# Attention scores ahead of two U/W tiles, eight PSUM banks in turn, and running sums ahead of the next scores

## The reference

```python
    k_all = jnp.concatenate([P['ak'], Pc['ak']], axis=1)
    o_att = _attend(P['aq'], k_all, v_all)          # softmax(q k' / 8) v
    o_dn, _, _ = _bidir_gdn(P, s_f, s_b)            # starts from the context's states

    # in _chunk_gdn, for chunks of 64 tokens
    u = einsum(tmat, vb)                            # tmat: inverse of (eye + lmat)
    w = einsum(tmat, kb * exp(gc))
    def step(S, inp):
        v_new = u_i - w_i @ S
        o = (q_i * exp(g_i)) @ S + qk_i @ v_new
        S = S * exp(g_last) + (k_i * exp(g_last - g_i)).T @ v_new
```

```python
        log_not = jnp.where(strict, jax.nn.log_sigmoid(-z), 0.0)
        after = lax.cumsum(log_not, axis=3, reverse=True) - log_not
        a = jnp.where(strict, jnp.exp(jax.nn.log_sigmoid(z) + after), 0.0)
        o = a @ v
```

## Time and profile before

| | |
|---|---|
| time, median of 3 runs | 1709.5 us (1709.14 to 1713.87) |
| profiled execution, its own time | 1710.61 us |
| its span in the trace | 1708.8 us |
| PE busy | 1543.9 us, 90% |
| DVE, ACT busy | 881.4 us (52%), 688.3 us (40%) |
| mean granted clock of TensorE | 0.901 |
| first block | 0 to about 640 us |
| loop of the attention and delta net | about 301 to 410 us |
| turns 7 to 11 of the two layers | 809 to 852 us, 1335 to 1381 us |

### The profile page before, as it was taken

How to read it: one execution, slowest core, us unless ns; L and a number is a source line. 1 busy time by engine, 2 the same in 40 slices (tenths; PEclk the granted TensorE clock), 3 DMA queues, 4 the chain that set the end, 5 groups by cost and what they waited for, 6 DMA issues and landing times. The chain is left out here.

```text
span 1708.8 us, 26973 instructions
## 1 busy us (share of the span) xinstructions
PE 1543.9 (90%) x11283; PEld 1305.1 (76%) x11283; DVE 881.4 (52%) x1330; ACT 688.3 (40%) x1141; POOL 75.6 (4%) x87
## 2 busy tenths in 40 slices
PE   4998889999799997989889899996989898899996
PEld 1555668666499997978787799986978787799984
DVE  0542643223455553467567555565448558555555
ACT  2112224323244442347662344453336664244442
POOL 0001661000000000000000000000000000000000
PEclk9888799556899997999999899998899998899998
DMA  9522154000445432622222755532642233555520
GB/s 357 203 70 78 38 198 165 1 1 1 173 172 190 177 101 81 197 99 99 99 99 99 295 196 178 177 125 74 181 159 67 83 119 128 214 200 180 193 99 25
DMA packets 118814, 230.34 MB, mean 135 GB/s; under 512 B 17984, under 2 KB 32448, under 8 KB 117952
## 3 DMA queue, kind: packets, MB, share of 16 engines
q1 hardware_dynamic: 115696, 221.37, 37.3%
q10 hardware_dynamic: 3024, 7.64, 1.2%
HBM read 227.95 MB, written 1.05 MB: 134 GB/s over the span
## 5 line engine op out<-in xcount | busy, mean ns | idle before, releaser
L707 DVE TENSOR_TENSOR work_rounded<-ring,work_rounded 128x1024 fp32r<-128x1024 f32 x208 | 240.8, 1220 | 113.7 <-ACT work_rounded L699 113.5
L670 PE MATMUL psum<-channels_rounded,work_rounded 128*128 128x256 f32 x2048 | 285.7, 286 | 0.9 <-DVE work_rounded L737 0.9
L670 PEld LDWEIGHTS psum<-channels_rounded,work_rounded 128*128 128x128 f32 x2048 | 271.6, 195 | 4.8 <-issue 3.4
L681 PE MATMUL psum<-work_rounded 128*128 128x512 f32 x1152 | 265.7, 390 | 0.0
L923 PE MATMUL psum<-channels_rounded,ring_rounded 128*128 128x256 f32 x1728 | 254.1, 291 | 3.0 <-DVE channels_rounded L1352 3.0
L699 ACT ACTIVATE work_rounded<-ring 128x1024 fp32r<-128x1024 f32 x208 | 203.2, 1050 | 131.7 <-PE psum L681 118.5
L681 PEld LDWEIGHTS psum<-work_rounded 128*128 128x128 f32 x1152 | 214.7, 188 | 43.6
L923 PEld LDWEIGHTS psum<-channels_rounded,ring_rounded 128*128 128x128 f32 x1728 | 230.7, 198 | 5.3 <-DVE channels_rounded L1352 3.8
L1344 DVE TENSOR_TENSOR ring_rounded<-ring,ring_rounded 128x1024 fp32r<-128x1024 f32 x80 | 94.4, 1195 | 61.0 <-ACT ring_rounded L1167 60.8
L1167 ACT ACTIVATE ring_rounded<-ring 128x1024 fp32r<-128x1024 f32 x80 | 80.6, 1024 | 24.3 <-DMA ring<-in_w_in 24.3
L747 DVE TENSOR_TENSOR work<-work 128x512 f32<-128x512 f32 x48 | 33.2, 692 | 109.7 <-ACT work L719 109.7
(11 more groups left out here) (358 smaller groups left out, 2158.6 us busy)
## 6 DMA issues: line engine op xcount, KB each, us to landing
ring<-in_w_in SPq DMA_DIRECT2D x20, 2048.0 KB, 7.8
ring<-in_w_ff SPq DMA_DIRECT2D x16, 2048.0 KB, 8.2
ring<-in_w_ff_in SPq DMA_DIRECT2D x16, 2048.0 KB, 8.0
ring<-in_w_ff_out SPq DMA_DIRECT2D x16, 2048.0 KB, 8.0
ring<-in_w_mod SPq DMA_DIRECT2D x12, 2048.0 KB, 8.6
ring<-in_w_out SPq DMA_DIRECT2D x6, 2048.0 KB, 8.7
ring<-in_w_in SPq DMA_DIRECT2D x8, 1024.0 KB, 5.4
ring<-in_w_up SPq DMA_DIRECT2D x4, 2048.0 KB, 8.0
```

The lines of the kernel that those rows point to most:

```text
L670: mm = pe.matmul(psum[:, 4 + 2 * half + q, i * SEQ:(i + 1) * SEQ], w1[pw][:, k, m * P:(m + 1) * P], y[py][:, k, :], start=((k, n) == (0, 0 ...
L681: mm = pe.matmul(psum[:, 2 * t + n, :], h[ph][:, kq, t * P:(t + 1) * P], w2[pw][:, kq, n * 512:(n + 1) * 512], start=False, stop=False, sk ...
L707: dve.tensor_tensor(parts.low[i % 2][:, at], ring[:, SLOT * s + 1024 * c:SLOT * s + 1024 * (c + 1)], exact(parts.high[i % 2][:, at]), ALU. ...
```

## The change

1. **Banks.** Every job of the first block up to the loop's last, that is all but the catA, catD, g and later ones, is added with `wide=True` and takes bank (4 + n) % 8. `Jobs` remembers who was in each bank last, and a job waits for that one: eight jobs back instead of four. The second block's jobs are as before.
2. **S_0.** The first scores, with the wait for the keys' copy, move on PE from behind the last W to behind the second tile's W, ahead of U and W of tiles 0 and 1. ACT's `probs(0)` moves likewise ahead of its copies of those four jobs. DVE's program is the same there.
3. **Stick-breaking turns.** In turns 7 to 11 the step T of the head before goes ahead of S of the next, on all three engines and in the order of the jobs. DVE's weights and their wait for the exponential move from step V to directly behind the addition in step T.

```diff
@@ class Jobs
+    def add(self, name, by, wide=False):
+        bank = (4 + len(self.all)) % 8 if wide else 4 + len(self.all) % 4
+        job = {"name": name, "n": len(self.all), "by": by, "k": self.counts[by], "bank": bank,
+               "old": self.in_bank.get(bank)}
+        self.in_bank[bank] = name
...
     def before(self, name):
-        n = self.by_name[name]["n"]
-        return self.all[n - 4]["name"] if n >= 4 else None
+        return self.by_name[name]["old"]
@@ first_jobs (every add up to PV15 has wide=True)
-    for t in TILES_D:
+    for n, t in enumerate(TILES_D):
+        if n == 2:
+            j.add("S0", "act", wide=True)
         add("act", f"U{t}", f"W{t}")
-    j.add("S0", "act")
@@ attention_schedule
     for n, (kind, h) in enumerate(HEADS + [(None, None)]):
+        swapped = last and last[:2] == "sb"
+        if swapped:
+            steps.append(("T", last))
         if kind:
             steps.append(("S", f"{kind}{h}"))
-        if last:
+        if last and not swapped:
             steps.append(("T", last))
@@ DVE, step T of a stick-breaking head (the same lines are gone from its step V)
                                     r.read(f"T_{name}", dve.tensor_tensor(b, b, ps, ALU.add))
+                                    dve.wait_ge(sb_exp, h + 1)
+                                    dve.scalar_tensor_tensor(out=b, in0=b, scalar=-1.0, in1=const_a("sb_neg"),
+                                                             op0=ALU.mult, op1=ALU.mult).then_inc(sb_weights, 1)
@@ PE, first block
                     for n, t in enumerate(TILES_D):
+                        if n == 2:
+                            w.after("akT")
+                            scores(0)
                         ps = w.open(f"U{t}")
...
-                    w.after("akT")
-                    scores(0)
                     for n in range(8):
@@ ACT, first block
+                    for n, t in enumerate(TILES_D):
+                        if n == 2:
+                            probs(0)
                         ps = r.open(f"U{t}")
...
-                    probs(0)
                     for n in range(8):
```

More of the change, by code:

```diff
@@ L145, in __init__ @@
         self.all, self.by_name, self.counts = [], {}, {"dve": 0, "act": 0, "gate": 0}
-    def add(self, name, by):
+        self.in_bank = {}
+    def add(self, name, by, wide=False):
         assert name not in self.by_name, name
-        job = {"name": name, "n": len(self.all), "by": by, "k": self.counts[by]}
+        bank = (4 + len(self.all)) % 8 if wide else 4 + len(self.all) % 4
+        job = {"name": name, "n": len(self.all), "by": by, "k": self.counts[by], "bank": bank,
+               "old": self.in_bank.get(bank)}
+        self.in_bank[bank] = name
         self.counts[by] += 1
@@ L154, in bank @@
     def bank(self, name):
-        return 4 + self.by_name[name]["n"] % 4
+        return self.by_name[name]["bank"]
     def full(self, name):
@@ L201, in add @@
         for name in names:
-            j.add(name, by)
+            j.add(name, by, wide=True)
     for u in range(4):
@@ L216, in first_jobs @@
     for kind, t in couplings_order():
-        j.add(f"{kind}{t}", "dve")
+        j.add(f"{kind}{t}", "dve", wide=True)
     for t in TILES_D:
-        j.add(f"LT{t}", "act")
+        j.add(f"LT{t}", "act", wide=True)
     add("act", "AT0", "AT1")
@@ L222, in first_jobs @@
         for t in TILES_D:
-            j.add(f"P{t}{lv}", "dve")
+            j.add(f"P{t}{lv}", "dve", wide=True)
         for n, t in enumerate(TILES_D):
             if lv == 5:
-                j.add(f"INV{t}", "act")
+                j.add(f"INV{t}", "act", wide=True)
                 continue
             if n % 2 == 0:
-                j.add(f"mod{2 + 2 * lv + n // 2}", "act")
+                j.add(f"mod{2 + 2 * lv + n // 2}", "act", wide=True)
             add("act", f"X{t}{lv}", f"XT{t}{lv}")
             if n % 2 == 0:
-                j.add(f"modT{2 + 2 * lv + n // 2}", "dve")
+                j.add(f"modT{2 + 2 * lv + n // 2}", "dve", wide=True)
     add("act", "aqT0", "aqT1", "aqT2", "aqT3", "akT")
-    for t in TILES_D:
+    for n, t in enumerate(TILES_D):
+        if n == 2:
+            j.add("S0", "act", wide=True)
         add("act", f"U{t}", f"W{t}")
-    j.add("S0", "act")
     for n in range(8):
         if n:
-            j.add(f"WS{n}", "dve")
+            j.add(f"WS{n}", "dve", wide=True)
         add("act", f"PT{2 * n}", f"S{2 * n + 1}")
-        j.add(f"SU{n}", "dve")
+        j.add(f"SU{n}", "dve", wide=True)
         if n >= 4:
@@ L245, in first_jobs @@
         if n < 7:
-            j.add(f"S{2 * n + 2}", "act")
-        j.add(f"PV{2 * n + 1}", "act")
+            j.add(f"S{2 * n + 2}", "act", wide=True)
+        j.add(f"PV{2 * n + 1}", "act", wide=True)
     for n in ("catA0", "catA1", "catD", "g0_0", "g0_1", "g1_0", "g1_1"):
@@ L1964, in _, with scores @@
                     w.done(mm)
+                    def scores(i):
+                        h, t = i // 2, i % 2
+                        kvh = half(h // 4)
+                        w.done(pe.matmul(w.open(f"S{i}"), v3(qT1, SEQ)[kvh, h % 4, t * P:(t + 1) * P], kT1[kvh, :],
+                                         start=True, stop=True))
                     for n, t in enumerate(TILES_D):
+                        if n == 2:
+                            w.after("akT")
+                            scores(0)
                         ps = w.open(f"U{t}")
@@ L1980, in _ @@
                         w.done(mm)
-                    def scores(i):
-                        h, t = i // 2, i % 2
-                        kvh = half(h // 4)
-                        w.done(pe.matmul(w.open(f"S{i}"), v3(qT1, SEQ)[kvh, h % 4, t * P:(t + 1) * P], kT1[kvh, :],
-                                         start=True, stop=True))
                     def probs_T(i):
@@ L2225, in _ @@
                     copy("akT", kT1)
-                    for t in TILES_D:
-                        ps = r.open(f"U{t}")
-                        for d in range(2):
-                            for p_ in range(2):
-                                last = act.activation(U_step[step_of[t, d, p_]][half(p_), :],
-                                                      ps[half(p_), 256 * d:256 * d + 256], ACT.Copy)
-                        r.read(f"U{t}", last)
-                        copy(f"W{t}", WT[t])
                     def probs(i):
@@ L2245, in values @@
                         r.read(f"PV{i}", act.mul(aq3[:, t, h * HD:(h + 1) * HD], r.open(f"PV{i}", HD), rden[:, i:i + 1]))
-                    probs(0)
+                    for n, t in enumerate(TILES_D):
+                        if n == 2:
+                            probs(0)
+                        ps = r.open(f"U{t}")
+                        for d in range(2):
+                            for p_ in range(2):
+                                last = act.activation(U_step[step_of[t, d, p_]][half(p_), :],
+                                                      ps[half(p_), 256 * d:256 * d + 256], ACT.Copy)
+                        r.read(f"U{t}", last)
+                        copy(f"W{t}", WT[t])
                     for n in range(8):
```

5 lines of the change are left out of this document (removed).

## The result

| | before | after |
|---|---|---|
| median of four executions | 1711.6 us (1709.14 to 1713.87) | 1661.5 us (1635.31 to 1684.89) |
| profiled execution, its own time | 1710.61 us | 1635.31 us |
| its span | 1708.8 us | 1633.5 us |
| mean granted clock | 0.901 | 0.940 |
| ratio, 95% interval | | 0.9572 (0.953 to 0.9614) |

What parts the groups turned out to be the heart of the matter. Six more executions of the same file, beside the kernel before on another chip, gave 1645.5 once, and 1672 to 1685 five times.

What follows compares the result with a forecast made beforehand. The loop was taken as bound by PE at half clock after a 1.95 us entry hole; 1710.61 - 4.4 (banks) - 43.5 (loop) - 13 (turns) = 1649.7, as a median 1649, range 1641 to 1693.

Steps and rivals of the forecast that it cites:

- rival (a): Loop's entry: the clock falls there all the same, only 2.9 us won; 1689, 1682 to 1697; chance 0.28.
- the turns' term: Stick-breaking turns 7 to 11, both layers: T and weights ahead of the next scores save 13 us, bounds 5 and 16.
- The loop (-43.5): Loop of attention and delta net: full clock from a shorter entry hole brings catD 43.5 us sooner, bounds 37 and 49.
- the loop isn't PE's any longer: Loop at full clock: latency of 3.7 us a head-tile, not PE's 3.1, sets turns of 7.4 us.
- The entry: Loop's start: S_0 earlier turns the 1.95 us hole into 0.5 to 0.6, taken not to lower the clock.
- The rule: Skill's claim that transposes don't engage the full clock; by it the loop, a sixth transposes, could fall to the lower level.
- the lift that I had put against the rule: Twelve transposes at 167.92 to 170.74, followed by a clock of 0.84 from 170 to 175, read as transposes alone raising it.
- Rival (c): Stick-breaking turns give nothing, DVE's new wait eating PE's gain; 1662, or 1702 with the low-clock loop; chance 0.07.
- The banks (-4.4): Inverse's third level ahead of the loop: eight banks let mod8 run under DVE's masking, 4.4 us less, lower bound 2.6.

Runs made afterwards that it cites:

- e1: Kernel before with two unused matmuls of 64x512 between S_0 and its wait for the exponential; median 1671.5 us against 1704.4, ratio 0.9801.
- e12: Kernel before with one unused matmul of 64x512 in the hole behind S_0; ten executions, 1701 to 1715 us, ratio 0.9989.
- e5: Kernel before with the eight banks alone, S_0 and turns as before; 1706.3 us against 1708.4, ratio 0.9995.
- e3: Changed kernel without the new order of the stick-breaking turns; 1664.5 us, and 1699.8, 1702.2 and 1704.5.
- e14: Changed kernel with a matmul of 64x256 behind SU_0, ahead of PV_0, the 0.45 us hole kept; 1640.5 us once, five of six in the upper group.
- e8: Changed kernel with a 64x256 filler ahead of SU_0 and six 128x512 matmuls in the 6.75 us hole ahead of 161; 1642.1 us, ratio 0.9613.
- e4: Changed kernel with one more matmul of 64x256 in the 0.45 us hole ahead of SU_0; 1639 to 1648 us, ratio 0.9639.
- e6: Kernel before with S_0's new place alone, four banks; 1673.1 us, and 1699.9, 1706.1 and 1719.3.
- e10: Changed kernel as it is, submitted a second time; 1645.5 us once, 1672 to 1685 five times.
- e2: Kernel before with the new order of the stick-breaking turns alone; 1685.3 us against 1704.4, ratio 0.9873.
- e7: Changed kernel with DVE's stick-breaking weights left in step V, only T ahead of S; three of four at 1665 to 1670 us, the fourth 1703.
- e9: Changed kernel with SU_0 waiting for the copy of W_3, not W_1; lower group 1643 to 1645 us, ratio 0.9614, two of six in the upper group.
- e11: Changed kernel with four banks and SU_0 waiting for W_3, not W_1; lower group 1648 to 1649 us, ratio 0.9640, three of six in the upper group.

## Why the prediction was right and wrong

- **What is measured against it.** The forecast was 1649, range 1641 to 1693. The median of the four executions, 1661.5, lies in the range and is the mean of two things that happen, not a thing that does. The lower group, by the ratio 0.9572 x 1709.5 = 1636, lies below the range; the upper, 1682 to 1685, is rival (a), which I had at 1689.
- **Against the fast group the sum was short.** The profiled execution, 1635.3, is 14.4 us below the 1649.7 of the sum. The step that failed there is the turns' term: 13 where 20.4 were measured. 6.6 more lie ahead of 146, a stretch that the sum put at nothing. The other terms hold: the banks and what follows up to S_0 4.0 for 4.4, the loop 44.1 for 43.5, the rest 0.2 for nothing.
- **The loop (-43.5): size right, the limit wrong.** 44.1 in the trace, by catD less what was won ahead, and the last wait is DVE's chain ahead of catD, 3.20 us, as named. The cause, the clock and the hole of 1.95 us, is shown by e1 and e12: filled, 1.00; 1.09 us of it left, ten of ten at the old time. But "the loop isn't PE's any longer" is not so. I had halved PE's turn, 12.45 to 6.2, and let the chain from scores to transposes set 7.4. The turn came as 7.12, of which PE is busy for 6.98; not 85% but 97% of the loop, with no recorded wait for the exponential. The chain comes out at 3.56 a head-tile, not 3.7: the transposes start 2.99 us behind their scores, 0.23 behind the exponential, the same distance as at the entry, where PE did wait for it. So both limits meet within some 0.1 us a turn, and that 7.4 was near 7.12 is partly luck. The heavy turns are as worked out (8.07 to 8.22 for 8.1).
- **The entry: a step that failed.** "A hole of 0.6 should not bring it, and I take that." The hole came out as 0.45, and by the times the clock fell in 7 of 10 executions. The row on which the step rested, a hole of 1.21 us lived through at 265, does show that such a hole can be harmless, as 1.66 us in e5 do; it didn't show that it is so at the entry, and e3 and e14 show that it isn't. What makes the one place differ from the other isn't shown. Rival (a) named it, "because it is the thin work there and not the hole alone, or because 0.6 us still do it", and had 0.28 where at least a half was due. A forecast of one number for a time that comes in two groups should have said so: either outcome, some 40 us apart, by a toss.
- **Transposes and the clock.** The rule was that of the Trainium skill ("TensorE: Matmul & The Clock Gate", "Part 4: PE-mode transpose"). The loop at 1.00, a sixth of whose work is transposes, isn't pulled down by them. And the lift that I had put against the rule was no single case. In twelve of the fifteen traces without e8 the clock is at 1.00 within 0.4 us of the end of the twelve transposes behind the long wait, before TensorE has done anything else; in after, e4 and e6 it stays at 0.50. During these transposes and behind them, in e10 (to 168.72) and in after (to 164.16):

```profile
166.00:168.50 2.50, 2.50 (x12) 2.32 (x12) 0.00 (x0) 1.13 (x2) 0.00 (x0) 0.50 0.00 0
169.00:169.40 0.40, 0.00 (x0) 0.00 (x0) 0.00 (x0) 0.40 (x2) 0.00 (x0) 1.00 0.00 0
161.50:164.00 2.50, 2.50 (x12) 2.26 (x12) 0.00 (x0) 1.19 (x2) 0.00 (x0) 0.50 0.00 0
164.20:164.80 0.60, 0.00 (x0) 0.00 (x0) 0.00 (x0) 0.54 (x2) 0.00 (x0) 0.50 0.00 0
```

So the rule, as the page puts it, doesn't hold in this case, and the rise is not certain either. In e8 the same twelve transposes kept the full pace (1.09 and 0.60).

- **The turns (-13): the mechanism right, the term mis-sized.** 8.6 and 11.8 us in after's trace, 19 to 22 in e2. Two things make up nearly all of the 7.4 between 13 and 20.4. I had worked out 15 and kept 13. The five turns take 34.0 us a layer where I had 36.5, which is 5 in all, most of it from the one-gate turns: I had DVE's round as their bound, 6.9, and they take 5.88 with PE busy for nearly all of it. I had laid the exponential, the next head's three operations and the gate's piece out one behind the other from each T, though DVE begins the next addition 1.24 us into the turn and PE waits only 0.30 us for DVE. What the old order costs also depends on the clock it gets, 42.7 to 48.2 us a layer, so the gain differs from execution to execution. Rival (c), that DVE's wait eats the gain, fell with e2; e7 shows that the gain needs the move of the weights, whose new wait I weighed against the change.
- **The banks (-4.4): right in the traces.** The wait and the slow product are gone as forecast, and the stretch is 4.4 us shorter over nine traces against six. The ratio of e5, 0.9995 (0.9973 to 1.0018), doesn't show it and doesn't exclude it; between e9 and e11, the same kernel with eight and with four banks on one chip, lie some 3.5 us, within the intervals.
- **What I hadn't in the sum.** 6.6 us up to 146 in the profiled execution of after: the clock took other levels there (0.91 before and 1.00 after from 120 to 160). That is not shown to be the change's: the same 32 matmuls of 128x256 start at 138.91 in after and at 145.48 in before, but at 141.30, 146.31 and 146.57 in e4, e9 and e8, whose first block has the same banks, and at 143.64 and 146.39 in e1 and e12.

## What to carry to other kernels

Where a stage runs at the lower clock though TensorE is busy all through, look at its first microseconds: a wait of one or two microseconds there can bring the whole stage to half pace, and a useless matmul in the wait cost nothing here and shows at once whether that is so. When a change is to save the clock, ask for a margin and time several executions: the outcome may otherwise be a toss. Put the fill into or ahead of the thin place, not behind it. Don't halve TensorE's time for twice the clock: take each group's time from rows at the upper level. When an engine has a chain's last step queued behind work that is in no hurry, move that step up with its wait; moving the step before it alone gave nothing here. And when whole executions scatter by more than a term is worth, compare the stretch that it changes over all traces.

## What the runs showed of the hardware

- At the loop's start, after a hole of 1.95 or 1.09 us the clock fell every time by the executions' times, in all those of the kernel before and ten of ten of e12; at 0.45 us it fell in 19 of 28, over five kernels that are the same at this place up to SU_0 but for the bank numbers; with 0.18 us left, in 5 of 12; with half a microsecond of matmul in its place, in none of 15. Elsewhere, a hole of 1.66 us among matmuls of 64x64 passed at 1.00 (e5).
- The fall can lag the hole: behind 2.07 us of idle time in e5, transposes (0.63) and scores (1.12) still ran at the full pace and the 64x64 matmuls behind them at half (1.45).
- Once at 0.50 the loop stayed there for its whole length although TensorE was 98.6% busy; the same loop at 1.00 is 97% busy (53.62 of 55) and stays at 1.00.
- Twice the clock gave 44 of the loop's 109 us and not 54. Groups of 16 matmuls of 64x64 went only from 1.38 to some 0.90 us where scores of 64x512 went from 2.00 to 1.05, and the chain of DVE and GpSimd behind the last turn took 7.6 us as before (349.51 to 357.07).
